# Routing, experts and combination as one stage; the first panel's low halves by VectorE; the first attention head loaded under the gate projection

## What is computed

```python
h = rmsnorm(x, norm_pre_g); z = h @ w_in                  # first projection: q, k, v, gate, convolution inputs
q, k = rope(q), rope(k)                                   # then banded attention of three dilations per head
...
g_idx = argmax(xt @ w_rg + b_rg)                          # one group of 8 experts per token, of 4
top_v, top_i = top_k(e_logits of that group, 2)           # two experts in it
gate = p_g * softmax(top_v)
dest = start of the expert's padded blocks + rank of the token in it   # blocks of 128 rows, one expert each
out_buf = [silu(xb @ w1[e]) * (xb @ w3[e]) @ w2[e] for each block]
y = sum over the two choices of gate * out_buf[dest]
out = rmsnorm(x + y, norm_f_g)
```

## Time and profile before

| | |
|---|---|
| median of 3 timed runs | 2792.05 us (2788.85 to 2793.62) |
| profiled execution, its own time | 2792.35 us |
| span in its profile | 2790.5 us |
| busy TensorE, VectorE, ScalarE, GpSimd | 2565.1, 1328.6, 1183.5, 634.0 us |
| mean granted TensorE clock | 0.966 |
| DMA | 455.78 MB, mean 163 GB/s |

### The profile page before, as it was taken

How to read it: one execution, slowest core, us unless ns; L and a number is a source line. 1 busy time by engine, 2 the same in 40 slices (tenths; PEclk the granted TensorE clock), 3 DMA queues, 4 the chain that set the end, 5 groups by cost and what they waited for, 6 DMA issues and landing times. The chain is left out here.

```text
span 2790.5 us, 30843 instructions
## 1 busy us (share of the span) xinstructions
PE 2565.1 (92%) x12104; PEld 2082.2 (75%) x12104; DVE 1328.6 (48%) x1716; ACT 1183.5 (42%) x1709; POOL 634.0 (23%) x520
## 2 busy tenths in 40 slices
PE   7999988879999999999998879999985999999992
PEld 6888866668787888878887668785774888888881
DVE  5530217764213212145424643105126888888885
ACT  4212227763241212123323522334213877777772
POOL 2312303323221313141301542354101111111100
PEclk9999999999999999999998989999986999999996
DMA  5433145523310131142215522441344999999995
GB/s 177 151 117 106 46 103 134 134 61 130 104 61 31 46 121 61 61 109 82 91 61 181 166 98 83 140 154 61 131 161 161 381 380 377 381 377 378 372 367 197
DMA packets 168690, 455.78 MB, mean 163 GB/s; under 512 B 17920, under 2 KB 85664, under 8 KB 155872
## 3 DMA queue, kind: packets, MB, share of 16 engines
q1 hardware_dynamic: 117856, 384.98, 38.3%
q10 hardware_dynamic: 37760, 41.17, 4.3%
q0 software_dynamic: 12928, 27.63, 2.8%
HBM read 389.23 MB, written 82.31 MB: 169 GB/s over the span
## 5 line engine op out<-in xcount | busy, mean ns | idle before, releaser
L2673 DVE TENSOR_TENSOR ex_w_lo<-ex_w,ex_w_hi 128x2048 fp32r<-128x2048 f32 x198 | 448.1, 2290 | 83.6 <-ACT ex_w_hi L2618 81.8
L2618 ACT ACTIVATE ex_w_hi<-ex_w 128x2048 fp32r<-128x2048 f32 x198 | 378.9, 1915 | 53.3 <-PEq L2219 26.4
L219 POOL TENSOR_TENSOR p_w_lo<-w_raw,p_w_hi 128x512 fp32r<-128x512 f32 (+1 forms) x154 | 203.3, 1352 | 632.2 <-ACT p_w_hi L239 607.2
L219 POOL TENSOR_TENSOR p_w_lo_rest<-w_raw,p_w_hi_rest 128x512 fp32r<-128x512 f32 x94 | 125.3, 1367 | 254.0 <-ACT p_w_hi_rest L239 254.0
L264 PE MATMUL o_ps<-o_w_hi,o_m_hi 128*128 128x512 f32 x384 | 154.6, 403 | 11.0 <-DVE split_cols L1175 11.0
L266 PE MATMUL o_ps<-o_w_hi,split_cols 128*128 128x512 f32 x384 | 152.9, 398 | 0.0
L265 PE MATMUL o_ps<-o_w_lo,o_m_hi 128*128 128x512 f32 x384 | 152.8, 398 | 0.0
L264 PE MATMUL p_ps<-p_w_hi,hT_hi 128*128 128x512 f32 (+1 forms) x320 | 120.8, 378 | 0.0
L266 PE MATMUL p_ps<-p_w_hi,hT_lo 128*128 128x512 f32 (+1 forms) x320 | 118.5, 370 | 0.0
L2485 POOL DMA_INDIRECT ex_x<-xn_rows,slot_token x33 | 36.1, 1093 | 362.0 <-PE ex_px L2532 327.0
L265 PE MATMUL p_ps<-p_w_lo,hT_hi 128*128 128x512 f32 (+1 forms) x320 | 118.1, 369 | 0.0
(11 more groups left out here) (475 smaller groups left out, 6463.0 us busy)
## 6 DMA issues: line engine op xcount, KB each, us to landing
ex_w<-w SPq DMA_DIRECT2D x99, 2048.0 KB, 13.9
w_raw<-w_in SPq DMA_DIRECT2D x42, 1024.0 KB, 5.1
x_rows<-o_x SPq DMA_DIRECT2D x24, 512.0 KB, 2.6
att_k<-k_columns SPq DMA_DIRECT2D x46, 256.0 KB, 7.6
w_raw<-w_out SPq DMA_DIRECT2D x8, 1024.0 KB, 9.6
qk_columns<-qk_y ACTq DMA_DIRECT2D x16, 512.0 KB, 2.6
o_x<-x_rows SPq DMA_DIRECT2D x16, 512.0 KB, 3.7
w_raw<-w_xkv SPq DMA_DIRECT2D x8, 1024.0 KB, 6.0
```

Of the source, the lines that this page charges most:

```text
L219: emit(self.lo(n)[:, 0:w], self.half(n // (KC // 2), w)[:, n % (KC // 2), :], self.hi(n)[:, 0:w].bitcast(F32), ALU.subtract).then_inc(self ...
L2618: nc.scalar.activation(w_hi[:, n % RING, :], raw_half(n), ACT.Copy).then_inc(hi_done, 1)
L2673: nc.vector.tensor_tensor(w_lo[:, n % RING, :], raw_half(n), w_hi[:, n % RING, :].bitcast(F32), ALU.subtract).then_inc(down_lo if m == "w2 ...
```

## The change

- **First panel.** VectorE takes the low halves of the first eight chunks, between the low halves of token tiles 0 and 1. ScalarE squares both first tiles and keeps tile 0's high half before any weight, then rounds all eight chunks, then keeps tile 1's. GpSimd begins with chunk 8.
- **First head.** A new class `HeadBuffers` holds head 0's q, k, the mask and both value buffers from the first projection on; q, k and the mask lie where the convolution's `conv_z` was, and the values' buffers serve the v projection. SyncE, at the end of its program there, waits for the stores and the convolutions and loads head 0. SyncE alone loads the other heads.
- **Routing.** The block around it is gone: its five programs run at the head of the experts' programs, without `retire_semaphores`. The sum over tiles is one scan, the table `before` holds what this asks for (minus one), ranks of both choices go together, the index search loses one step, the table's one-hots are fp32r in four quarters with a semaphore for each, the table gives token and row in 96 columns, and steps that the table doesn't need stand behind it. The first low halves of the experts and the rows' low half change order.
- **Combination.** Its programs run at the tail of the experts'. ScalarE waits for the scatters and releases SyncE; results are loaded into free weight buffers.

The diff, cut (`...` where lines are left out; of the routing only what is new):

```diff
+    c["before"][:] = (p[:, None] < p[None, :]) - 1.0
...
+class HeadBuffers:
+
+
+
+    def __init__(self, c, stack):
+        nc = c.nc
+        with nc.sbuf_tensor("conv_z", [P, 4, S], F32) as self.conv_z:
+            pass
+        self.spare = stack.enter_context(nc.sbuf_tensor("att_first", [P, 3, S], F32R))
+        self.logc = stack.enter_context(nc.sbuf_tensor("logc", [P, S], F32))[:, :]
+        self.v_rows = stack.enter_context(nc.sbuf_tensor("att_v", [P, 2, 2 * BANK], F32R))
+        self.v = self.v_rows[:, :, :].rearrange("p b (t d) -> p b t d", t=NT)
...
+                for b in range(2):
+                    sp.wait_ge(qk_out[b], 32 * n_qk // 2)
+                    sp.wait_ge(lo_out[b], 32 * n_qk // 2)
+                    sp.wait_ge(v_out[b], 16 * (n_v - n_qk) // 2)
+                sp.wait_ge(conv_done, CW // P)
+                for half in range(2):
+                    heads.load_qk(sp, 0, half, q_dram, k_dram)
+                sp.dma_start(heads.logc, c.const_dram("logc")).then_inc(heads.logc_in, 16)
+                heads.load_v(sp, 0, v_dram)
...
-                weights.take_los(pool)
+                pool.wait_ge(weights.lo_done, KC)
+                weights.take_los(pool, (KC, weights.n_chunks))
...
-                for t in range(NT):
+                scale_rows(0)
+                scale_rows(1)
+                take_low_rows(0)
+                for n in range(KC):
+                    weights.take_lo(dve, nc.vector.tensor_tensor, n)
+                take_low_rows(1)
+                for t in range(2, NT):
                     scale_rows(t)
-                    if t >= 1:
+                    if t >= 3:
                         take_low_rows(t - 1)
...
                 measure_rows(0)
-                take_high_weights(0, 2)
                 measure_rows(1)
                 take_high_rows(0)
-                take_high_weights(2, 8)
+                take_high_weights(0, KC)
+                take_high_rows(1)
                 for t in range(2, NT):
                     measure_rows(t)
-                    take_high_rows(t - 1)
+                    if t >= 3:
+                        take_high_rows(t - 1)
                     if t == 4:
                         take_high_weights(KC, weights.R)
...
-                for b in range(2):
-                    act.wait_ge(qk_out[b], 32 * n_qk // 2)
-                    act.wait_ge(lo_out[b], 32 * n_qk // 2)
-                    act.wait_ge(v_out[b], 16 * (n_v - n_qk) // 2)
...
-                for h in range(NH):
+                for h in range(1, NH):
                     if h >= 2:
                         sp.wait_ge(scored, NT * (h - 1))
-                    load_head(sp, h, 0)
-                    if h >= 1:
-                        load_head(sp, h, 1)
-                    b = h % 2
+                    for half in range(2):
+                        heads.load_qk(sp, h, half, q_dram, k_dram)
                     if h >= 2:
                         sp.wait_ge(summed, 12 * (h - 1))
-                    sp.dma_start(vs[:, b, :, :].bitcast(F32), v_dram[:, h * P:(h + 1) * P
-                                                                    ].rearrange("(t p) d -> p t d", p=P)
-                                 ).then_inc(v_in[b], 16)
+                    heads.load_v(sp, h, v_dram)
                     if h == 1:
...
-                pool.dma_start(logc[:, :], c.const_dram("logc")).then_inc(logc_in, 16)
...
-                load_head(act, 0, 1)
...
+        def route_sp(sp):
+            expert_weights.load(sp, 0, up=False)
+            expert_weights.load(sp, 1)
+
+        def route_pool(pool):
+            nc.gpsimd.memset(xg[:, :, :], 0.0).then_inc(cleared, 1)
+            pool.wait_ge(cleared, 1)
+            pool.wait_ge(slots, 1)
+
+        def route_pe(pe):
+            pe.wait_ge(chosen, 1)
+
+            pe.matmul(pk[:, 0, :, :], c.const("before"), oh[:, :, :], start=True, stop=True)
+            pe.matmul(pn[:, 0, :, :], c.const("ones"), oh[:, :, :], start=True, stop=True).then_inc(ranked, 1)
+            for i in range(2 * NT):
+                k, t = 1 - i // NT, i % NT
+                if i % 4 == 0:
+                    pe.wait_ge(placed, i // 4 + 1)
+                ins = pe.matmul(pt[:, 0:2 * NBLK], d1[:, k * NT + t, :], d2[:, k, t, :, :].rearrange("p a b -> p (a b)"),
+                                start=(i == 0), stop=(i == 2 * NT - 1))
+            ins.then_inc(tabled, 1)
...
+            def first_of_max(values, n, top, onehot, iota, spare, idx=idx[:, :]):
+
+                step(V.tensor_reduce(top[:, :], values, AX, ALU.max))
+                step(V.tensor_tensor(spare, values, bc(top[:, :], n), ALU.not_equal))
+                step(V.scalar_tensor_tensor(spare, spare, 64.0, iota, ALU.mult, ALU.add))
+                step(V.tensor_reduce(idx, spare, AX, ALU.min))
+                step(V.tensor_tensor(onehot, iota, bc(idx, n), ALU.is_equal))
+
+            V.memset(d2[:, 0, :, 1, :].bitcast(F32), 0.0)
+            step(V.memset(fresh[:, :, :], 1.0))
+            step(V.memset(fresh[:, :, 0:1], 0.0))
+            step(V.tensor_tensor(lg[:, :, :], pl[:, :, 0:NR], bias[:, :].unsqueeze(1).to_broadcast([P, NT, NR]), ALU.add))
...
+            V.tensor_tensor(oh[:, :, :].rearrange("p e t -> p t e"), oh1, oh2, ALU.add).then_inc(chosen, 1)
...
+            dve.wait_ge(ranked, 1)
+            step(V.tensor_tensor_scan(counts[:, :, :].rearrange("p e t -> p (e t)"),
+                                      fresh[:, :, :].rearrange("p e t -> p (e t)"),
+                                      pn[:, 0, :, :].rearrange("p e t -> p (e t)"), 0.0, ALU.mult, ALU.add))
+            step(V.tensor_scalar(cnt_i[:, :], counts[:, :, NT - 1], float(P - 1), None, ALU.add))
...
+            step(V.tensor_tensor(seen[:, :, :], pk[:, 0, :, :], counts[:, :, :], ALU.add))
+            step(V.tensor_tensor(wide[:, :, :, :], both[:, :, :, :],
+                                 seen[:, :, :].rearrange("p e t -> p t e").unsqueeze(1).to_broadcast([P, 2, NT, NE]),
+                                 ALU.mult))
+            step(V.tensor_reduce(rank[:, :, :], wide[:, :, :, :], AX, ALU.add))
+            step(V.tensor_tensor(wide[:, :, :, :].rearrange("p k t e -> p (k t) e"),
+                                 both[:, :, :, :].rearrange("p k t e -> p (k t) e"),
+                                 move[:, :].unsqueeze(1).to_broadcast([P, 2 * NT, NE]), ALU.mult))
+            step(V.tensor_reduce(over[:, :, :], wide[:, :, :, :], AX, ALU.add))
+            step(V.scalar_tensor_tensor(over[:, :, :], rank[:, :, :], float(P), over[:, :, :], ALU.is_ge, ALU.mult))
+            step(V.scalar_tensor_tensor(rank[:, :, :], idx12[:, :, :], float(P), rank[:, :, :], ALU.mult, ALU.add))
+            step(V.tensor_tensor(dest_f[:, :, :], rank[:, :, :], over[:, :, :], ALU.add))
...
+            for k in range(2):
+                ins = V.tensor_tensor(d2[:, k, :, k, :], c.const("blk").unsqueeze(1).to_broadcast([P, NT, NBLK]),
+                                      hi[:, k, :].unsqueeze(2).to_broadcast([P, NT, NBLK]), ALU.is_equal)
+            step(ins)
+            for k in range(2):
+                V.scalar_tensor_tensor(d2[:, k, :, 0, :], c.const("tokid").unsqueeze(2).to_broadcast([P, NT, NBLK]),
+                                       1.0, d2[:, k, :, k, :].bitcast(F32), ALU.add, ALU.mult)
+            for i in range(4):
+                k, t = 1 - i // 2, i % 2 * (NT // 2)
+                V.tensor_tensor(d1[:, k * NT + t:k * NT + t + NT // 2, :],
+                                c.const("iota").unsqueeze(1).to_broadcast([P, NT // 2, P]),
+                                lo[:, k, t:t + NT // 2].unsqueeze(2).to_broadcast([P, NT // 2, P]), ALU.is_equal
+                                ).then_inc(placed, 1)
+
+            dve.wait_ge(tabled, 1)
+            step(V.tensor_scalar(none[:, :], pt[:, 0:NBLK], 0.5, float(NOWHERE), ALU.is_lt, ALU.mult))
+            V.scalar_tensor_tensor(slot_token[:, :], pt[:, 0:NBLK], -1.0, none[:, :], ALU.add, ALU.add
+                                   ).then_inc(slots, 1)
+            step(V.scalar_tensor_tensor(row[:, :], pt[:, NBLK:2 * NBLK], float(S), none[:, :], ALU.mult, ALU.add))
+            step(V.scalar_tensor_tensor(slot_row[:, :], pt[:, 0:NBLK], -1.0, row[:, :], ALU.add, ALU.add))
+            step(V.tensor_tensor(cmp[:, :, :], pend[:, :].unsqueeze(1).to_broadcast([P, NEXTRA, NE]),
+                                 c.const("blk")[:, 0:NEXTRA].unsqueeze(2).to_broadcast([P, NEXTRA, NE]), ALU.is_le))
+            step(V.tensor_reduce(be[:, :], cmp[:, :, :], AX, ALU.add))
+            step(V.tensor_scalar(extra_expert[:, :], be[:, :], float(NE - 1), None, ALU.min))
+            step(V.tensor_scalar(nb[:, :], pend[:, NE - 1:NE], 1.0 / P, -1.0, ALU.mult, ALU.add))
+            step(V.tensor_scalar(n_rest[:, :], nb[:, :], 0.0, None, ALU.max))
...
-        w_hi, w_lo = sb("w_hi", [P, RING, HALF], F32R), sb("w_lo", [P, RING, HALF], F32R)
```

(20 more changed lines are left out.)

356 lines of the change are left out of this document (154 added, 202 removed).

## The result

The changed kernel takes 2757.45 us (median of four runs, 2754.62 to 2760.14), the kernel before, timed beside it, 2790.45 (2785.80 to 2793.62). The ratio is 0.9882 with an interval of 0.9868 to 0.9896: 33.0 us faster where 33.2 were forecast, at 2759. The profiled run took 2760.14, its span 2758.3, mean granted clock 0.972 (before 0.966).

What follows compares the result with a forecast made beforehand. TensorE, busy 92% of the span, was taken as the bound, with gains only at four places where it waits. 3.1 + 11.3 + 12.3 + 6.5 = 33.2 us off 2792.35 gave 2759, range 2753 to 2769.

Steps and rivals of the forecast that it cites:

- R1: End of experts: the loop over extra blocks takes 8.5 us on every engine, combination gains only 1.9; 2763.7 us; chance 0.14.
- R2: First head: head 1's transfer takes the wait's place, gain there 9.0; 2761.4 us, 2763 with low clock; chance 0.09.
- R3: Routing table: fp32r matmuls are no cheaper, routing loses 4.2 us; 2763.3 us; chance 0.07.
- R4: Expert stage: swapped SBUF places make VectorE's conversions dearer, kernel slower beyond 20.5%, 2801 us at 22%; chance 0.02.
- R5: Whole kernel: the change does nothing, as clears or loads stay where they are; 2792 us; chance 0.02.
- Part A: First panel at the start: token tile 2 is transposed earlier, 3.1 us off, bounds 0.5 and 4.0.
- It meets no missing chunk: First panel: TensorE's first group, from 16.6 to 22.55 us, finds every weight chunk ready.
- the new wait of 0.9: First panel: TensorE waits about 0.9 us for tile 2, whose rows ScalarE and VectorE finish late.
- Part B: First projection to attention: head 0's loads hidden under the gate projection, 11.3 us gained, bounds 8 and 13.6.
- Part C: Routing, from last router score to first expert matmul: 12.3 us gained, bounds 7 and 13.6.
- behind them stand four fp32r matmuls: Routing table: after VectorE's last digits at 4.6 us only four matmuls of 0.22 remain, done at 5.5; gain 5.8.
- Part D: Last expert to combination: ScalarE releases the loads without a barrier, 6.5 us gained, bounds none and 6.7.

Runs made afterwards that it cites:

- e4_fp32_table: The changed kernel with the one-hots of the routing table in fp32 in place of fp32r; 2759.81 us.
- e6_busy_pe: The changed kernel with TensorE multiplying constants into an unused bank while it waits in the routing, results never read; median 2755.45 us.

## Why the prediction was right, and where it was not

**Forecast against rivals.** 2759 was right and no rival's condition came true. R1: the loop is about equally long on both engines, as R1 has it, but 1.9 us on GpSimd and 2.1 on ScalarE, not 8.5, and the loads came 2.66 behind the scatter, not 8. R2: head 1's keys were waited for, 2.36 us in place of the 0.6 I took, between the forecast and R2's 2.9, and the stretch it belongs to came out 0.7 below the forecast; R2 said 2.3 below. R3: refuted by e4_fp32_table. R4: the expert stage is as long as before, 610.60 against 610.42, its VectorE share 438.86 against 437.97 in 500 us. R5 is excluded by the result.

**Part A, 3.1 forecast, 2.7 measured.** In the profiled run, nearly the right sum by a wrong way. "It meets no missing chunk" held, and ScalarE waited 1.63 for the second half of the panel as it had to. But the group of 24 matmuls, which I took as 5.95 long, took 7.46 (16.82 to 24.28), where before it took 6.36 (20.19 to 26.55). The passes start 0.43 apart until 20.8, nine of them; before, the clock rose at 21.6, when only three had run. Starting 3.4 us earlier, six more passes ran at half speed, 1.2 us. And so the new wait of 0.9 for tile 2's scaling never showed: the scaled row was ready at 23.50, before TensorE asked. This holds for this run alone. In the changed kernel's second profile the clock rose after three passes, the group took 6.67, and TensorE did wait 0.24 for the scaling; tile 2 came 12.67 behind the first transposes, which is 3.5 off before's 16.21. Over all profiles that keep both halves of A the distance is 12.6 to 13.5, a gain of 2.75 to 3.6 with the forecast's 3.1 inside; before has one profile only.

**Part B, 11.3 forecast, 10.6 measured.** The idle time fell from 11.69 to 0.94, as said (10.75). The failed terms are the two small ones behind it. The clock was kept at first, and the first 16 passes took 3.86 in place of 5.79, 1.9 won where I had 1.2. But TensorE then waited 2.36 for head 1's keys, not 0.6, and behind that wait the clock fell all the same, to 0.50 in the window 400 to 402. The six loads took 9.5 us from the first issue (388.65 to 398.13), not 8.4, and TensorE asked 7.1 us behind its first score, not 7.75. So the transfer sets when head 1 starts, and a faster start of head 0 only lengthens the wait. The two terms together came out at -0.2 (10.55 less 10.75) in place of +0.6; counted at the last head (203.1 to 192.0) they are +0.3, and the half microsecond between is in the last head's own time.

That a pause of 1 us keeps the clock is not certain either. In two of the eight profiles it fell behind the same pause, the changed kernel's second profile among them (window), and the 16 passes took 4.9 and 5.0. The wait for head 1's keys was then 0.68 and 0.81, head 1 started no later than in the others (10.3 and 10.4), and the clock did not fall there:

```profile
392.00:394.00 2.00, 2.00 (x9) 1.82 (x8) 1.45 (x3) 0.92 (x2) 0.00 (x0) 0.50 1.02 219
```

**Part C, 12.3 forecast, 10.85 measured.** By its steps: the stage change and clears 0.94 (1.0 forecast); everything from VectorE's first routing step to the digit steps 3.6 (22.65 to 19.06; 4.05 forecast); the table 4.9 (11.33 to 6.39; 5.8 forecast); from the table to the first expert matmul 1.4 (1.4 forecast). The 0.45 lacking in the second is covered by two steps that I took at the price of plain ones: the one-hots written with tokens innermost took 0.62 in place of 0.42, and the product that reads them back across took 1.08 in place of 0.69. The three memsets took 0.87, not 0.7; the additions gave 0.2 more than forecast. The scan took 0.22 us over 32 elements and 0.69 over 256, plain steps 0.19 and 0.42: 2.1 ns against 1.0 for each further element. The rule of the Trainium skill ("DVE: opcode table, instruction layouts, handler registers and perf-mode slots", Feedback) that the built-in scan runs at half throughput agrees with it. The 0.9 in the table is the term I priced by VectorE, "behind them stand four fp32r matmuls": at 0.213 each TensorE falls behind by 0.2 us a quarter, and the sixteen end 3.65 behind their start, 1.9 behind VectorE's last digit.

**Part D, 6.5 forecast, 7.2 measured.** Nearly the right size, by luck, for a wrong reason (and above the bound of 6.7). I took the loop for the length, 8.5 us on GpSimd, and thought ScalarE would be through it sooner. GpSimd, which issued its scatter at 2740.39, was at its last loop step at 2744.14, and then drained for 5.46 us. The forecast held because both reasons end with the same rule: let nobody wait for GpSimd's end. For a release placed on GpSimd my reason would have said that all of D is lost; the loads came 2.91 behind the scatter, and in the kernels that release from ScalarE 2.66 to 3.10.

**The rest.** 31.3 us are the change's by these parts (2.7 + 10.6 + 10.85 + 7.2); the 0.9 that is left of the profiled 32.2 is clock scatter less the late start. The medians' 33.0 agrees within the spread of either kernel, 5 to 8 us. That it comes so near to 33.2 is partly luck: the parts are 1.9 us short of their forecasts (A, B and C by 2.6 together, D over by 0.7), and the medians lie 1.7 above the parts.

## What to carry to other kernels

Price the end of a stage by the record of each engine's queue, not by the work that stands before it: a drain on GpSimd was over half of the gap between the last scatter and the loads behind it (5.46 of 9.76 us), and a semaphore in place of the barrier, from ScalarE or from GpSimd itself, took the loads out from behind it. Read what a moved transfer gives at the end of the stage that it feeds, not at the next wait: of 2.3 us at the second head 1.2 were left at the last. Ask of every earlier start at which clock it now runs, and compare single profiles stretch by stretch: a low-clock stretch that one run has and the other lacks is worth 1.5 us here.

## What the runs showed of the hardware that I had not expected

- GpSimd's drain at the end of the expert stage took 5.46 us before, 5.55 us after and 5.46 to 5.59 in the other runs, with its indirect transfers landed; in the changed kernel too it runs, from 2718.72, but nothing waits for it. What it does in that time no run shows. Drains at the ends of other stages of the same kernel took 1.2 to 3.8 us, beside TensorE's work.
- A VectorE tensor-scalar step over 32 elements was held until GpSimd's fill of 2048 elements ended (0.72 us in place of 0.17); in the kernel before, one over 8 elements took 0.41 beside the same fill and ended with it (2086.23 and 2086.20). Two-operand steps and reductions beside it were not held.
- In the router scores TensorE is shown busy without a gap, 2.00 of 2.00 us, and the granted clock is 0.50 all the same (window of the changed kernel); in e6_busy_pe it fell at the end of the table's matmuls, with no idle time longer than 1.15 us in the 20 us ahead:

```profile
2064.00:2066.00 2.00, 2.00 (x12) 2.00 (x11) 0.00 (x0) 0.00 (x0) 0.00 (x0) 0.50 0.00 0
```

- Two profiled runs of the changed kernel have spans of 2758.3 and 2752.7; 3.0 of the 5.6 us lie in the experts, where one of them has two stretches of 3.4 us at 1.2 GHz that the other lacks.
